# First norm of a two-layer decoder kernel: load order, diagonal products and split work at the start

## What is computed

```
def rmsnorm(x, g):
    xf = x.astype(jnp.float32)
    y = xf * lax.rsqrt(jnp.mean(xf * xf, axis=-1, keepdims=True) + EPS)
    return (y * g.astype(jnp.float32)).astype(x.dtype)
...
for l in range(DEPTH):
    h = rmsnorm(x, norm1_g[l])
    x = x + mixing_block(h, cos, sin, w_in[l], sgu_ln_g[l], ...)
    h = rmsnorm(x, norm2_g[l])
    x = x + hier_moe(h, w_group[l], ...)
```

## Time and profile before

| what | value |
|---|---|
| time before, median of 3 runs | 768.95 us (768.6 to 770.28) |
| the profiled execution's own time | 770.31 us |
| its span, first to last instruction | 768.5 us |
| PE busy | 757.3 us, 99% of the span |
| DVE, ACT, POOL busy | 636.6, 499.4, 22.6 us |
| moved by DMA | 180.57 MB, mean 235 GB/s |

### The profile page before, as it was taken

One profiled execution on the slowest core, in us unless ns is written; L12 is line 12 of the kernel. 1 busy time (PEld: TensorE's weight loads), 2 busy tenths in 40 slices (PEclk: granted clock), 3 DMA queues, 4 the chain that ended last, 5 costly groups with the idle time before them and its releaser, 6 DMA issues.

```text
span 768.5 us, 12928 instructions
## 1 busy us (share of the span) xinstructions
PE 757.3 (99%) x4786; PEld 679.1 (88%) x4786; DVE 636.6 (83%) x855; ACT 499.4 (65%) x592; POOL 22.6 (3%) x42
## 2 busy tenths in 40 slices
PE   7999999999999999999999999999999999999997
PEld 7899999999878888888799999999988888888885
DVE  4858899469779998989775789956977999898995
ACT  7535566645588877777662546565548878776773
POOL 4030000000000000000001000000000000000000
PEclk9999999999999999999999999999999999999999
DMA  9866345356727999999465553534764499999961
GB/s 308 279 220 219 112 165 165 100 201 247 253 76 267 335 382 361 353 357 320 129 219 168 200 182 119 184 111 145 266 225 159 159 353 358 375 360 333 338 241 55
DMA packets 86418, 180.57 MB, mean 235 GB/s; under 512 B 13238, under 2 KB 25176, under 8 KB 86360
## 3 DMA queue, kind: packets, MB, share of 16 engines
q1 hardware_dynamic: 86360, 179.79, 67.2%
HBM read 178.72 MB, written 1.05 MB: 234 GB/s over the span
## 4 chain that ended last, share of the span: by engine, by line
PE 96%; DVE 1%; ACT 1%; issue 1%; DMA 1%; POOL 0%; DVEq 0%; ACTq 0%; POOLq 0%
PE bank L1511 28%; PE bank L1513 28%; PE bank L1512 28%; PE bank L1909 2%; PE bank L1827 2%; PE bank L1797 1%; PE bank L1935 1%; PE bank L1676 1%; PE bank L1581 1%; DMA x<-in_x 1%; PE bank L1584 0%; PE bank L1790 0%; ACT gates L586 0%; PE bank L2003 0%; PE bank L1561 0%
## 5 line engine op out<-in xcount | busy, mean ns | idle before, releaser
L916 DVE TENSOR_TENSOR w_lo<-raw,w_hi 128x2048 fp32r<-128x2048 f32 (+1 forms) x140 | 304.5, 2194 | 54.8 <-ACT w_hi L563 54.2
L563 ACT ACTIVATE w_hi<-raw 128x2048 fp32r<-128x2048 f32 (+1 forms) x140 | 256.1, 1841 | 127.6 <-PE bank L1513 126.9
L1511 PE MATMUL bank<-a_hi,w_hi 128*128 128x256 f32 x688 | 196.2, 285 | 0.6 <-DVE a_lo L981 0.6
L1512 PE MATMUL bank<-a_hi,w_lo 128*128 128x256 f32 x688 | 195.0, 283 | 0.0
L1513 PE MATMUL bank<-a_lo,w_hi 128*128 128x256 f32 x688 | 195.0, 283 | 0.0
L1511 PE MATMUL bank<-w_hi,y_lo 128*128 128x512 f32 x408 | 161.7, 396 | 0.0
L1513 PE MATMUL bank<-w_lo,y_lo 128*128 128x512 f32 x408 | 159.4, 391 | 0.0
L1511 PEld LDWEIGHTS bank<-a_hi,w_hi 128*128 128x128 f32 x688 | 132.2, 192 | 1.6 <-issue 1.5
L1512 PEld LDWEIGHTS bank<-a_hi,w_lo 128*128 128x128 f32 x688 | 132.2, 192 | 0.1
L1513 PEld LDWEIGHTS bank<-a_lo,w_hi 128*128 128x128 f32 x688 | 132.2, 192 | 0.0
L1512 PE MATMUL bank<-w_hi,y_hi 128*128 128x512 f32 x272 | 106.2, 391 | 0.0
(11 more groups left out here) (331 smaller groups left out, 960.9 us busy)
## 6 DMA issues: line engine op xcount, KB each, us to landing
raw<-in_w_gate SPq DMA_DIRECT2D x56, 512.0 KB, 4.7
raw<-in_w_e_gate SPq DMA_DIRECT2D x42, 512.0 KB, 4.6
raw<-in_w_e_up SPq DMA_DIRECT2D x42, 512.0 KB, 6.3
mid<-in_w_e_down SPq DMA_DIRECT2D x36, 512.0 KB, 6.2
raw<-in_w_in SPq DMA_DIRECT2D x32, 512.0 KB, 6.0
raw<-in_w_e_gate SPq DMA_DIRECT2D x40, 256.0 KB, 4.5
raw<-in_w_e_up SPq DMA_DIRECT2D x40, 256.0 KB, 5.4
mid<-in_w_e_down SPq DMA_DIRECT2D x40, 256.0 KB, 5.2
```

Source lines behind the costliest of these rows:

```text
L563: a.activation(w_hi[:, at.part(n), 0:w], raw_at(slot)[:, 0:w], ACT.Copy).then_inc(hi_done, at.count(n))
L916: v.tensor_tensor(w_lo[:, part, 0:w], raw_at(slot)[:, 0:w], w_hi[:, part, 0:w].bitcast(F32), ALU.subtract).then_inc(split_done, at.count(n))
L1511: mm(ps, a2[0], b2[0], start=first, stop=False, skip_group_check=shared)
L1512: mm(ps, a2[1], b2[0], start=False, stop=False, skip_group_check=shared)
```

## The change

The norm's weights are requested ahead of unit 0. SP then waits until unit 0 has landed, loads unit 1, requests the positions and the 14 mixer parameters, and only then loads units 2 and 3; the router's parameters follow. Half 0 of the tokens is no longer scaled by DVE and transposed: DVE copies it unscaled, makes a diagonal matrix of `rs1`, and PE multiplies each block with it, which scales and transposes in one. Half 1 is scaled by DVE alone. DVE also makes `h_hi` of channel blocks 0 and 1. The products of ones are 11 and 4 in place of 14 and 6. The second layer's instructions stay as they are.

```
--- before.py
+++ after.py
@@ -419,13 +419,15 @@
                 for n in range(n0, AHEAD):
                     load(at, n, *units_a[n], l)
 
+            norm_gains(0)
             load(At(0, 0, False), 0, *units_a[0], 0)
-            norm_gains(0)
-            first_units(At(0, 0, False), 0, 1)
-            load(At(0, 0, False), AHEAD, *units_a[AHEAD], 0)
+            sp.wait_ge(landed[0], 16 * DMAS)
+            load(At(0, 0, False), 1, *units_a[1], 0)
             sp.dma_start(posi[:, :], positions[0].rearrange("(t p) -> p t", p=P),
                          allow_slow_non_contiguous=True).then_inc(pos_loaded, 16)
             mixer_parameters(0)
+            first_units(At(0, 0, False), 0, 2)
+            load(At(0, 0, False), AHEAD, *units_a[AHEAD], 0)
             router_parameters(0)
             sp.wait_ge(S("tab_zero"), 1)
             for l in range(DEPTH):
@@ -585,17 +587,16 @@
                 act.wait_ge(x_loaded[t], 16)
                 a.activation(sq_dump[:, t, :], x[:, t, :], ACT.Square, scale=float(D ** -0.5),
                              accum_out=ssqh[:, t, 0:1]).then_inc(S("n1_ssq"), 2)
-            scale_part(0)
             hi(At(0, 0, False), 0)
             act.wait_ge(S("tab_zero"), 1)
             for l in range(DEPTH):
                 act.wait_ge(par_g, 16 * (l + 1))
-                for k in range(KT):
+                for k in range(0 if l else 2, KT):
                     act.wait_ge(S("n1_t"), 4 * l + k % 4 + 1)
                     if k >= 4:
                         act.wait_ge(S("h_lo_done"), KT * l + k - 3)
                     a.activation(h_hi[:, k, :], bank[4 + k % 4][:, 256 * (k // 4):256 * (k // 4) + 256], ACT.Identity,
-                                 scale=g1[:, k:k + 1]).then_inc(S("h_hi_done"), 1)
+                                 scale=g1[:, k:k + 1]).then_inc(S("h_hi_done"), 3 if l == 0 and k == 2 else 1)
                 before = act.value_load(tab[0:1, 0, 9:10], min_val=0, max_val=DEPTH * MAXP) if l else 0
                 at = At(l, before, False)
                 if l == 0:
@@ -935,15 +936,30 @@
             v.tensor_copy(tab[:, :, :], tab_f[:, :, :]).then_inc(S("tab_zero"), 1)
 
             def rstd_rows(l):
-                for t in range(T):
+                def mean_square_in(t):
                     dve.wait_ge(S("n1_ssq"), 2 * T * l + (t + 3 if l else 2 * t + 2))
                     v.tensor_scalar(ms1[:, t:t + 1], ssqh[:, t, 0:1], ssqh[:, t, 1:2], EPS, ALU.add,
                                     ALU.add).then_inc(S("n1_ms"), 1)
-                for t in range(T):
+
+                def scaled(t, k):
                     dve.wait_ge(S("n1_rs"), T * l + t + 1)
-                    k = 4 * t
                     v.tensor_scalar(xn[:, t, k:, :], x[:, t, :].rearrange("q (p c) -> q c p", c=KT)[:, k:, :],
                                     rs1[:, t:t + 1], None, ALU.mult).then_inc(S("n1_x"), 1)
+
+                if l == 0:
+                    dve.wait_ge(pool_consts, 3)
+                    dve.wait_ge(x_loaded[0], 16)
+                    v.tensor_copy(xn[:, 0, :, :], x[:, 0, :].rearrange("q (p c) -> q c p", c=KT)).then_inc(S("n1_x"), 1)
+                    mean_square_in(0)
+                    dve.wait_ge(S("n1_rs"), 1)
+                    v.tensor_scalar(diag[:, 0, :], ident[:, :], rs1[:, 0:1], None, ALU.mult).then_inc(S("n1_d"), 1)
+                    mean_square_in(1)
+                    scaled(1, 0)
+                else:
+                    mean_square_in(0)
+                    mean_square_in(1)
+                    scaled(0, 0)
+                    scaled(1, 4)
 
             rstd_rows(0)
 
@@ -977,7 +993,14 @@
 
             for l in range(DEPTH):
                 for k in range(KT):
-                    dve.wait_ge(S("h_hi_done"), KT * l + k + 1)
+                    if l == 0 and k < 2:
+                        dve.wait_ge(par_g, 16)
+                        dve.wait_ge(S("n1_t"), k + 1)
+                        v.tensor_scalar(h_hi[:, k, :], bank[4 + k][:, 0:256], g1[:, k:k + 1], None,
+                                        ALU.mult).then_inc(S("h_hi_first"), 1)
+                        dve.wait_ge(S("h_hi_first"), k + 1)
+                    else:
+                        dve.wait_ge(S("h_hi_done"), KT * l + k + 1)
                     v.scalar_tensor_tensor(out=h_lo[:, k, :], in0=bank[4 + k % 4][:, 256 * (k // 4):256 * (k // 4) + 256],
                                            scalar=g1[:, k:k + 1], in1=h_hi[:, k, :].bitcast(F32),
                                            op0=ALU.mult, op1=ALU.subtract).then_inc(S("h_lo_done"), 1)
@@ -1527,18 +1550,31 @@
             pe.wait_ge(pool_consts, 3)
             pe.wait_ge(S("tab_zero"), 1)
             for l in range(DEPTH):
-                keep_warm(4, 16 if l else 14)
-                for t in range(T):
-                    pe.wait_ge(S("n1_x"), T * l + t + 1)
-                    if t:
-                        pe.wait_ge(S("n1_xa"), l + 1)
-                    for k in (0, 4, 1, 5, 2, 6, 3, 7):
-                        c = 256 * (k // 4) + P * t
-                        last = tp(bank[4 + k % 4][:, c:c + P], xn[:, t, k, :], ident[:, :])
-                        if t == T - 1 and k >= 4:
-                            last.then_inc(S("n1_t"), 1)
+                keep_warm(4, 16 if l else 11)
+
+                def turned_at(t, k):
+                    c = 256 * (k // 4) + P * t
+                    return bank[4 + k % 4][:, c:c + P]
+
                 if l == 0:
-                    keep_warm(3, 6)
+                    pe.wait_ge(S("n1_x"), 1)
+                    pe.wait_ge(S("n1_d"), 1)
+                    for k in range(KT):
+                        mm(turned_at(0, k), xn[:, 0, k, :], diag[:, 0, :], start=True, stop=True, skip_group_check=True)
+                    pe.wait_ge(S("n1_x"), T)
+                    for k in range(4):
+                        tp(turned_at(1, k), xn[:, 1, k, :], ident[:, :])
+                        tp(turned_at(1, k + 4), xn[:, 1, k + 4, :], ident[:, :]).then_inc(S("n1_t"), 1)
+                    keep_warm(3, 4)
+                else:
+                    for t in range(T):
+                        pe.wait_ge(S("n1_x"), T * l + t + 1)
+                        if t:
+                            pe.wait_ge(S("n1_xa"), l)
+                        for k in (0, 4, 1, 5, 2, 6, 3, 7):
+                            last = tp(turned_at(t, k), xn[:, t, k, :], ident[:, :])
+                            if t == T - 1 and k >= 4:
+                                last.then_inc(S("n1_t"), 1)
 
                 before = pe.value_load(tab[0:1, 0, 9:10], min_val=0, max_val=DEPTH * MAXP) if l else 0
                 at = At(l, before, False)
```

## The result

The changed kernel takes 772.91 us (772.1 to 774.6, 6 runs) against 769.73 (768.6 to 770.28, 6 runs) for the kernel before: 3.2 more. The ratio on record is 1.0046 with a 95% interval of 1.0036 to 1.0056 (the two medians alone make 1.0041). It is slower, by somewhat more than the forecast 2.3. The profiled execution took 772.7, its span 770.9.

A forecast was written before the change was run, and what follows sets the result against it. PE was taken to bound the kernel (96% of the chain), the rest mostly the start. Gain 1.7 at the start, waits 1.75 and 2.25 at units 2 and 4: 2.3 slower, 768.95 to 771.3 us, range 768.2 to 775.2.

The forecast's parts named there:

- The start: Norm up to PE's first product of `w_in`: 11.3 instead of 13.02, a gain of 1.7, at least 0.85.
- The queue of SP: Units 2 and 3 behind unit 0's landing, positions and parameters: unit 2 issued at 16.8, landed at 22.25.
- PE and the angles: PE waits 1.75 before unit 2 and 2.25 before unit 4, the latter behind unit 3's rest, angles and GELUs.
- the one-line form: Unit 4 on PE moves from 37.55 to unit 2's landing time plus 17.6, whatever the start gains, once landing exceeds 19.9.
- Slow parameters: Rival: SP issues positions and 14 parameters as slowly as before (1.10, 9.7); 775.3. Chance 0.18, shared with a falling clock.
- Unit 2 early enough: Rival: unit 2 lands under 18.2, issued at 12.7, so the start's full gain survives; 767.3. Chance 0.08.
- A norm without gain: Rival: POOL's second `rs1` stays 1.39 or the diagonal is slow; start gains 0.85, sum stays 2.3. No separate chance.
- The falling clock: Rival: PE's clock falls in the new waits, costing up to 2.0; 773.3. Chance 0.18, shared with slow issues.
- the sum against the median: Whole kernel: gain 1.7 against waits 1.75 and 2.25, 2.3 slower, added to the before median of 768.95.

The follow-up runs named there:

- the transfers alone: The kernel before with SP's new order of transfers and the old norm: 772.94 us, ratio 1.0041.
- the early angles: The changed kernel with the angles moved on DVE ahead of unit 2's rest, the sine on ACT ahead of unit 2's rounding: 773.38 us, ratio 1.0061.
- unit 2 first: The changed kernel with unit 2 issued straight after unit 1, only unit 3 left behind positions and parameters: 773.79 us, ratio 1.0052.
- without the wait for unit 0: The changed kernel without SP's wait for unit 0's landing, positions and parameters still ahead of units 2 and 3: 770.0 us, ratio 1.0002.
- the first kernel: The changed kernel with SP's old order of transfers, so only the norm's part of the change: 768.23 us, ratio 0.998.
- both orders of units: The changed kernel with unit 2, or units 2 and 3, issued ahead of positions and parameters: 773.79 us (ratio 1.0052) and 774.25 us (1.0071).
- the nine products: The changed kernel with 9 products of ones on PE ahead of unit 4: 774.0 us, ratio 1.0062.
- products in both waits: The changed kernel with products of ones, 6 ahead of unit 2, 8 ahead of unit 4 and 14 for 11 at the start: 773.05 us, ratio 1.0041.
- 2.4 with the early angles: The changed kernel with angles ahead of unit 2's rest, plus 8 products of ones ahead of unit 2 and 14 at the start: 771.88 us, ratio 1.0026.

## Why the prediction was right

**The start: right.** First product forecast 11.3, measured 11.26; POOL's second `rs1` forecast 0.55, measured 0.55; the diagonal forecast 0.3, measured 0.28; the 16 records of diagonal products forecast 1.8, measured 2.02 to their last end. The norm alone shows that it gains 1.5 (median) to 1.9 (at unit 4) where nothing takes it. That a GpSimd and a VectorE operation of the two-port kind exclude each other (the Trainium skill, SBUF — State Buffer, "Who interferes with whom") agrees with the traces: 1.39 beside the scaling (before, and again with the transfers alone), 0.55 without it (after, and with the norm alone).

**The queue of SP: right in kind, and exact by luck.** Unit 0 landed at 9.25, not 8.7; the positions (0.47, forecast 0.55) and the parameters (5.52, forecast 6.5) were quicker. So unit 2 was issued at 16.30 and not at 16.8, but landed 5.95 behind its issue and not 5.45: at 22.25, as forecast, just ahead of 22.31, where ACT begins. Four errors of up to 1.0 cancel there.

**PE and the angles: right.** Waits forecast 1.75 and 2.25, measured 1.73 and 2.30. Angles begin at 29.61 (forecast 29.3), since unit 3 landed at 25.4 and not 25.0: one of the four issues of units 2 and 3 took 1.23 where the median is 0.47. Unit 4 at 40.12 (forecast 39.85). Unit 4's own transfers were issued at 26.09 and not at 21.7, since the router's three first parameters took 0.48, 1.80 and 3.63; that error cost nothing here, for the angles ended later still, but with the early angles it became the limit. The kernel with the transfers alone confirms the one-line form, that with unit 2 first shows that unit 3's landing and not unit 2's carries it on, and that with the early angles shows the chain: with the angles moved the GELUs end 0.85 earlier (39.21 for 40.06).

**The rivals.** Slow parameters: refuted at this place (5.52), though with more outstanding they are slow (8.55 without the wait). Unit 2 early enough: refuted, and the point from which it decides lies elsewhere than I put it, since unit 3 must be early as well. A norm without gain: refuted by the first kernel. The falling clock: not seen behind the waits in the profiled execution after (0.997 over all, 1.00 in each 10 us up to 50), but seen in others with such waits. The windows of the kernel with the transfers alone, behind its wait of 2.12:

```profile
39.50:41.50 2.00, 1.45 (x9) 0.79 0.80 252
41.50:43.50 2.00, 2.00 (x11) 0.50 0.76 252
43.50:45.50 2.00, 2.00 (x17) 0.86 0.04 12
```

There up to 1.7 us were lost (0.21, 0.50 and 0.14 of 2.0 each).

**The term that was mis-sized** is the sum against the median: 2.3 forecast, 3.2 measured. Unit 4's delay of 2.57 (40.12 - 37.55) holds 0.3 of the difference. The rest goes with the clock. Of the 71 executions of the kernel before in the sets of the experiments, 38 show a granted clock of 0.999 or more, with spans of 766.7 to 767.6; 29 show 0.996 to 0.998, with a median span of 768.2, and four 0.992, with 770.3 to 771.0. None of the 6 after, and none of the 8 with the transfers alone, shows over 0.998. At equal clock (0.996 to 0.998) the four spans after are 770.3 to 770.9, some 2.4 above before's 768.2, as the forecast has it (and the profiled execution, forecast at 772.6, took 772.7). The forecast median of 771.3 also started from 768.95, a median of three, where six executions of the kernel before give 769.73. The medians differ by 0.8 more, as I read it because the change has fewer executions without a fall. In the profiled execution after the fall lies in the first layer, between short products of its router; the windows after:

```profile
218.00:222.00 4.00, 3.69 (x20) 1.00 0.54 170
222.00:226.00 4.00, 4.00 (x19) 0.64 0.23 92
226.00:230.00 4.00, 4.00 (x19) 0.93 0.00 0
```

The profiled execution before has such a fall at 588 to 594, in the second layer's router. The experiments bear the reading out in part. Of the kernels with SP's wait for unit 0 and no products of ones ahead of unit 2 (the change, the transfers alone, both orders of units, the early angles, the nine products) not one of 38 executions shows 0.999 or more; with products ahead of unit 2 and 14 at the start it is 12 of 24, about as in the kernel before (which of the two does it was not run apart). In those 12 the span is above before's 767.0 by about what unit 4 is late: 3.2 with products in both waits (unit 4 3.1 later), 2.4 with the early angles (2.0 later). So the kernel with products in both waits got its executions without a fall back; that its median is still no lower than the change's goes at least in part with its unit 4, which came another 0.55 later. What is not shown is why the profiled execution after has its only fall at the router and none behind the head's waits; whether a wait in the head brings falls far behind it stays open.

## What to carry to other kernels

A place in the issuing queue is worth what the engines behind it do with the data, so follow a moved transfer through all of them: here the units that were moved back fed not only PE's next products; behind their rests on DVE the angles, the sine, two roundings and the GELUs stood in program order, and a part of the loss came out 14 us later at another unit. A gain at the start is only worth something if no landing further on sets the same point: ask of each half of a change what it does alone, and run the halves; here one was 1.5 faster and the other 3.2 slower, and together they were 3.2 slower too. When a wait is removed by reordering, look for the engine that then waits for what was put behind.

## What the runs showed of the hardware

- **The time of an issue on SP rose with what was outstanding.** The same 14 small transfers took 5.52 behind unit 1 (after), 7.1 with one more unit ahead (unit 2 first), 8.55 to 8.6 with units 0 and 1 outstanding (without the wait) or two more units ahead, and 9.7 in the kernel before, behind four units. The router's `b_group`, 2 KB, was issued in 0.58 in the kernel with the norm alone and in 3.63 after the change, where units 2 and 3 (2 MB) had gone out just ahead of it.
- **PE lost its clock behind some of its waits and not behind others, and the length of the wait does not tell which.** After waits of 1.22 (the nine products), 2.12, 2.46, 2.52 and 3.75 the granted clock was 0.50, which is 1.2 GHz, for part of what followed; after 1.50 (without the wait for unit 0) and after 1.73 and 2.30 (the change) it stayed at 1.00. The Trainium skill, TensorE: Matmul & The Clock Gate, "Part 1: The HAM clock gate", has an idle TensorE fall back to half rate; the traces agree for five of these eight waits.
- **The row of granted clock reads 1.00 over the first 10 us of each kernel**, though the first records of ones took 421 ns against 275 later. In the kernel with the nine products it reads 1.00 up to 12 us, over the 16 diagonal records of 421 ns. At the start the record's length tells the clock, the column does not.
